# Re-ordering the weight loads of the first expert stage: earlier pieces for one unit, 0.9 MB more room for another

## The reference, cut to what matters

```python
for e in range(N_EXPERTS):                       # 32
    hid = jax.nn.silu(hf @ w_gate[e]) * (hf @ w_up[e])      # 1024 -> 256, twice
    y = y + (hid @ w_down[e]) * combine[:, e:e + 1]         # 256 -> 1024
```

## Time and profile before

| | us |
|---|---|
| median of three runs | 777.58 |
| lowest, highest | 776.46, 778.38 |
| the profiled execution, its own time | 776.66 |
| its span in the trace | 774.8 |
| outside the span (776.66 less 774.8) | 1.86 |

### The profile page before, as it was taken

One profiled execution on the slowest core, in us unless ns is written; L12 is line 12 of the kernel. 1 busy time (PEld: TensorE's weight loads), 2 busy tenths in 40 slices (PEclk: granted clock), 3 DMA queues, 4 the chain that ended last, 5 costly groups with the idle time before them and its releaser, 6 DMA issues.

```text
span 774.8 us, 16731 instructions
## 1 busy us (share of the span) xinstructions
PE 720.2 (93%) x7452; PEld 458.9 (59%) x7452; DVE 324.6 (42%) x688; ACT 206.7 (27%) x418; POOL 31.5 (4%) x99
## 2 busy tenths in 40 slices
PE   8999999999989998999999999999998997877796
PEld 6778787658645564554537745885765553343342
DVE  7476886635353323333236064633355331221222
ACT  2574568215100000000042363530330000100003
POOL 7006000000000000000000000000000000000000
PEclk9999999999999999999999999999999998898999
DMA  8644113399999999999999724359589999999995
GB/s 257 211 89 160 57 57 112 144 418 418 384 422 417 422 419 420 420 420 421 413 346 360 249 76 172 135 193 370 209 325 420 417 421 420 420 422 421 420 405 190
DMA packets 74871, 241.62 MB, mean 312 GB/s; under 512 B 10087, under 2 KB 39901, under 8 KB 55726
## 3 DMA queue, kind: packets, MB, share of 16 engines
q1 hardware_dynamic: 74590, 240.00, 80.1%
q10 hardware_dynamic: 208, 0.54, 0.2%
HBM read 239.48 MB, written 1.05 MB: 310 GB/s over the span
## 4 chain that ended last, share of the span: by engine, by line
PE 59%; DMA 15%; DVE 4%; issue 1%; SPq 1%; ACT 0%; ACTq 0%
PE ps L1588 11%; PE ps L1911 10%; DMA M<-in_m_w_up_dram 8%; PE ps L1424 7%; PE ps L1525 7%; PE ps L1667 5%; PE ps L1540 4%; DMA M<-in_m_w_down_dram 4%; DMA M<-in_m_w_gate_dram 3%; DVE H L2525 1%; PE ps L1063 1%; PE ps L1733 1%; PE ps L1805 1%; PE ps L1533 1%; PE ps L1459 1%
## 5 line engine op out<-in xcount | busy, mean ns | idle before, releaser
L1588 PE MATMUL ps<-M 128*32 128x256 f32 x2008 | 122.8, 393 | 15.7 <-DMA M<-in_m_w_gate_dram 8.8
L1588 PEld LDWEIGHTS ps<-M 128*32 128x32 f32 x2008 | 65.1, 113 | 70.5 <-issue 15.7
L1117 PE MATMUL ps<-M 128*128 128x272 f32 x352 | 85.3, 397 | 0.6 <-DMA M<-in_e_w_in_dram 0.6
L1911 PE MATMUL ps<-M 128*128 128x256 f32 (+2 forms) x288 | 79.9, 434 | 0.0
L1525 PEld LDWEIGHTS ps<-M 128*128 128x128 f32 x608 | 72.3, 194 | 12.7 <-issue 12.2
L1525 PE MATMUL ps<-M 128*128 128x128 f32 x608 | 77.8, 280 | 0.0
L1117 PEld LDWEIGHTS ps<-M 128*128 128x128 f32 x352 | 65.6, 190 | 15.9 <-issue 1.7
L1667 PE MATMUL ps<-M 128*32 128x512 f32 x448 | 59.6, 679 | 10.6 <-DMA M<-in_m_w_down_dram 10.6
L1911 PEld LDWEIGHTS ps<-M 128*128 128x128 f32 x288 | 53.7, 190 | 22.6 <-issue 15.6
L1540 PE MATMUL ps<-M 128*128 128x512 f32 (+1 forms) x120 | 60.4, 625 | 5.4 <-DVE H L2525 5.4
L2522 DVE TENSOR_TENSOR H<-H,ps 128x512 f32<-128x512 f32 x60 | 41.3, 688 | 49.2 <-PE ps L1540 48.9
(11 more groups left out here) (467 smaller groups left out, 851.7 us busy)
## 6 DMA issues: line engine op xcount, KB each, us to landing
M<-in_m_w_gate_dram SPq DMA_DIRECT2D x28, 2048.0 KB, 17.9
M<-in_m_w_up_dram SPq DMA_DIRECT2D x22, 2048.0 KB, 20.3
M<-in_m_w_down_dram SPq DMA_DIRECT2D x19, 2048.0 KB, 22.7
M<-in_m_w_down_dram SPq DMA_DIRECT2D x14, 1024.0 KB, 16.5
M<-in_o_w_in_dram SPq DMA_DIRECT2D x12, 1024.0 KB, 9.5
M<-in_e_w_in_dram SPq DMA_DIRECT2D x11, 1024.0 KB, 5.8
M<-in_m_w_gate_dram SPq DMA_DIRECT2D x9, 1024.0 KB, 6.9
M<-in_m_w_up_dram SPq DMA_DIRECT2D x8, 1024.0 KB, 18.8
```

Of the source, the lines that this page charges most:

```text
L1117: ins = pe.matmul(ps[:, n % 4, 0:T], wringE[:, (n // 2) % 4, k, (n % 2) * P:(n % 2) * P + P], (xnE if n else xuE)[:, k], start=(k == 0), s ...
L1588: ins = pe.matmul(ps[32 * e:32 * e + 32, 3 * x, 0:FF], xgT[q % 2][:, k, 32 * e:32 * e + 32], w, start=(k == 0), stop=(k == KD - 1))
L1911: ins = pe.matmul(ps[rows, unit % 4, 0:n], lhs(k), rhs(k), start=(k == 0), stop=(k == KD - 1))
```

## The change

It changes loads of the first expert stage, and with them where three tensors lie and which counts the waits of TensorE look for.

- **Pieces.** Of unit 2 (down weights of round 0, place 3) the first two experts are sent as four transfers of 0.5 MiB, each behind `oc_set` 1, 2, 3, 4. The last two experts stay behind `sa_evac` 5 and `lru_in` 6, as one transfer of 2 MiB.
- **A place of 0.5 MiB.** `aside[0]` gets a fourth entry: the first half of the up weights of the fourth expert of round 1 goes there, right behind those 2 MiB; before it went into place 1 behind `half_done` 1.
- **A place of 0.4 MB.** The level masks (`m_lev`) and the router weights (`wrr`) become parts of the tensor `K1`, which grows by what they had. `first_cols` (768 columns, 0.375 MiB) lies over the masks and the first layer's router weights; a transfer into it waits for `wrc_set` 1 (the router weights have been scaled into their own tensor, DVE line 2340). It takes the first three of the eight k slices of the first expert of unit 1. The part of place 2 that is free by this takes 0.375 MiB of the down weights of round 1 (unit 5) behind `res_done` 5.
- **What follows.** Behind `half_done` 1 go 2 MiB of unit 4 in two transfers; behind `gate_done` 1 the second halves of unit 8 (2 MiB, before 1.5 MiB behind `up_done` 1); behind `half_done` 2 only 0.125 MiB of unit 5; behind `up_done` 1 its second halves (2 MiB). Unit 8's first halves go as two transfers of 1 MiB.

```diff
-        aside = [[K0[:, 0:D], K1[:, 0:D], yst[1]], ...
+        aside = [[K0[:, 0:D], K1[:, 0:D], yst[1], at(36096, D)], ...
+        first_cols = K1[:, 1024:1024 + 3 * FF]
 # but_quarters (unit 1)
-                    sp.dma_start(slots[j][:, 0, :], src[:, 0, :]).then_inc(s(f"ld_s{j}"), 16)
+                    sp.dma_start(slots[j][:, 0, 3 * FF:2 * D], src[:, 0, 3 * FF:2 * D]).then_inc(s(f"ld_s{j}"), 16)
 ...
                 if y == 0:
+                    for c in range(4):
+                        e, h = divmod(c, 2)
+                        sp.wait_ge(s("oc_set"), c + 1)
+                        sp.dma_start(slots[3][:, e, D * h:D * h + D], down[:, e, D * h:D * h + D]).then_inc(s("ld_s3"), 16)
                     sp.wait_ge(s("sa_evac"), NC)
                     sp.wait_ge(s("lru_in"), 6)
-                    whole(2, down[:, 0:4])
+                    sp.dma_start(slots[3][:, 2:4, :], down[:, 2:4, :]).then_inc(s("ld_s3"), 16)
+                    set_aside(3)
 ...
 # unit 1, behind mixE 5
                             for e in range(2):
                                 set_aside(e)
+                            sp.wait_ge(s("wrc_set"), 1)
+                            sp.dma_start(first_cols, up[:, 0, 0:3 * FF]).then_inc(s("ld_pv_ys"), 16)
 # unit 3, behind res_done 5
+                            sp.dma_start(slots[UNIT_SLOT[y][5]][:, 0, 0:3 * FF], down[:, 4, 0:3 * FF]).then_inc(s("ld_lruw_e5"), 16)
 # unit 4
                             sp.wait_ge(s("half_done"), 1)
-                            sp.dma_start(slots[j][:, 3, 0:D], up[:, 7, 0:D]).then_inc(s("ld_half"), 16)
-                            sp.dma_start(slots[j][:, 0:3, 0:D], up[:, 4:7, D:2 * D]).then_inc(s(f"ld_s{j}"), 16)
+                            for e in (0, 2):
+                                sp.dma_start(slots[j][:, e:e + 2, 0:D], up[:, 4 + e:6 + e, D:2 * D]).then_inc(s(f"ld_s{j}"), 16)
                             wait_through(UNIT_PREV[y][u])
-                            sp.dma_start(slots[j][:, 3, D:2 * D], up[:, 7, D:2 * D]).then_inc(s(f"ld_s{j}"), 16)
+                            sp.dma_start(slots[UNIT_SLOT[y][8]][:, :, D:2 * D], down[:, 8:12, D:2 * D]).then_inc(s("ld_u8_lastk"), 16)
 # unit 5
                             sp.wait_ge(s("half_done"), 2)
-                            sp.dma_start(slots[j][:, 0, 0:D], down[:, 4, 0:D]).then_inc(s(f"ld_s{j}"), 16)
+                            sp.dma_start(slots[j][:, 0, 3 * FF:D], down[:, 4, 3 * FF:D]).then_inc(s(f"ld_s{j}"), 16)
                             wait_through(UNIT_PREV[y][u])
-                            sp.dma_start(slots[j][:, 0:3, D:2 * D], down[:, 4:7, D:2 * D]).then_inc(s(f"ld_s{j}"), 16)
-                            sp.dma_start(slots[j][:, 3, D:2 * D], down[:, 7, D:2 * D]).then_inc(s("ld_lruw_e5"), 16)
-                            sp.dma_start(slots[UNIT_SLOT[y][8]][:, 0:3, D:2 * D], down[:, 8:11, D:2 * D]).then_inc(s("ld_u8_lastk"), 16)
+                            sp.dma_start(slots[j][:, :, D:2 * D], down[:, 4:8, D:2 * D]).then_inc(s(f"ld_s{j}"), 16)
 ...
 # TensorE, half_gu
+                            elif u == 1 and y == 0 and k < 3 and e == 0:
+                                w = first_cols[:, FF * k:FF * k + FF]
```

More of the change, by code:

```diff
@@ L111, in program @@
         hsel, E2, cen, onesbd = K0[:, 640:672], K0[:, 672:800], K0[:, 800:928], K0[:, 928:1056]
-        K1 = sb("K1", [P, 1152])
+        K1 = sb("K1", [P, 2112])
         reset, gupO = K1[:, 0:640].bitcast(BF16), K1[:, 640:1152]
@@ L118, in program @@
         iota = sb("iota", [P, P])
-        m_lev = sb("m_lev", [P, 6, L])
+        m_lev = K1[:, 1152:1536].rearrange("p (l t) -> p l t", l=6)
         pv = sb("pv", [P, NPV])
@@ L126, in program @@
         dlast = sb("dlast", [P, 4, NC])
-        wrr = sb("wrr", [P, 2, KD, NG + NE])
+        wrr = K1[:, 1536:2112].rearrange("p (y k c) -> p y k c", y=2, k=KD)
         wrc = sb("wrc", [P, KD, NG + NE])
@@ L290, in program @@
         level, cmp = at(31616, NE, 8), at(31616 + 8 * NE, 16, NE)
-        aside = [[K0[:, 0:D], K1[:, 0:D], yst[1]], [K0[:, 0:D], K1[:, 0:D], at(26624, D), yst[1]]]
+        aside = [[K0[:, 0:D], K1[:, 0:D], yst[1], at(36096, D)], [K0[:, 0:D], K1[:, 0:D], at(26624, D), yst[1]]]
         apart = [H[:, 2, :], xgT[1].rearrange("p k t -> p (k t)"), at(33792, D), yst[0]]
         spare = at(36096, D)
+        first_cols = K1[:, 1024:1024 + 3 * FF]
         fn_row, fnb = K1[0:1, 0:D], K0[:, 0:D]
@@ L476, in experts @@
                         if y == 0:
-                            sp.dma_start(slots[j][:, 0:3, 0:D], down[:, 8:11, 0:D]).then_inc(s(f"ld_s{j}"), 16)
-                            sp.dma_start(slots[j][:, 3, :], down[:, 11, :]).then_inc(s(f"ld_s{j}"), 16)
+                            for e in (0, 2):
+                                sp.dma_start(slots[j][:, e:e + 2, 0:D], down[:, 8 + e:10 + e, 0:D]).then_inc(s(f"ld_s{j}"), 16)
                         else:
@@ L1557, in loaded @@
                     j = UNIT_SLOT[y][u]
+                    more = 48 if j == 3 else 0
                     if y == 0:
-                        pe.wait_ge(s(f"ld_s{j}"), 32 * (UNIT_TURN[y][u] + 1))
+                        pe.wait_ge(s(f"ld_s{j}"), 32 * (UNIT_TURN[y][u] + 1) + more)
                     else:
-                        pe.wait_ge(s(f"ld_s{j}"), 32 * FIRST_LAYER[j]
+                        pe.wait_ge(s(f"ld_s{j}"), 32 * FIRST_LAYER[j] + more
                                    + 16 * sum(TRANSFERS.get(x, 2) for x in range(u + 1) if UNIT_SLOT[1][x] == j))
                     if u == 1:
-                        pe.wait_ge(s("ld_pv_ys"), (304, 368)[y])
+                        pe.wait_ge(s("ld_pv_ys"), (320, 384)[y])
                     elif y == 0 and u == 3:
@@ L1581, in half_gu @@
                                 w = aside[y][e][:, FF * k:FF * k + FF]
-                            elif u == 4 and k >= KD // 2 and e < 3:
+                            elif u == 4 and k >= KD // 2 and (y == 0 or e < 3):
                                 w = gu_w[UNIT_SLOT[y][u]][:, e, k - KD // 2, :]
-                            elif u == 4 and k >= KD // 2 and y == 1:
+                            elif u == 4 and k >= KD // 2:
                                 w = spare[:, FF * (k - KD // 2):FF * (k - KD // 2) + FF]
+                            elif u == 1 and y == 0 and k < 3 and e == 0:
+                                w = first_cols[:, FF * k:FF * k + FF]
                             elif u == 1 and k < KD // 2 and e + y:
```

## The result

The changed kernel took 780.60 us (median of 18 runs, 777.72 to 785.71), the kernel before 777.53 (18 runs beside it, 776.04 to 780.38): a ratio of 1.0038 with a 95% interval of 1.0023 to 1.0053. It is slower, by 3.07 us, where 0.95 us faster was forecast, and the time lies outside the forecast range of 774.5 to 778.8.

The account below looks back on a forecast made before the run. Two paths were taken to end the first expert stage together: the weight stream and TensorE's own work. Removing waits of 0.75 and 0.20 us gives -0.95; 777.58 - 0.95 = 776.6 us, range 774.5 to 778.8.

Parts of the forecast that it names:

- So 2 MiB go into idle time: Chunk loop, 132 to 147 us: four pieces, 1.25 us each at 418 GB/s, fit where only 4 GB/s move.
- The mechanism: Rival, chance 0.08: four instruction loads at 132 to 147 us meet pieces, TensorE runs dry, up to 5.0 us lost.
- The argument against it: Against the instruction-load rival: from 150 to 195 us, at 418 GB/s, TensorE was busy 44.05 of 45 us.
- The fixed cost of 2 us a transfer: Skill page's cost beside the bytes; in the stream, four more transfers would cost 8 us. Restart rival: 782.6, chance 0.04.
- the lead: Weight stream of the first expert stage runs ahead by 1.7 to 2.6 us; 2.0 taken.
- The hole: Gap in the stream near 195 us, places full and waiting for TensorE; to grow from about 0.8 to 3.7 us.
- -0.95 us: Last round of the first expert stage: TensorE's waits for gate (0.75) and second half of up weights (0.20) go.
- No place is waited for longer: Behind the hole near 195 us, the changed byte order makes no wait for a place longer; nothing charged.
- TensorE's start at 193 us unmoved: Sign of being right: TensorE's expert work still starts at 193 us; later than 193.5 would be wrong.
- The second limit: Issue at 313.99 us, behind slow gate matmuls (6.26 instead of 3.66 us), caps the lead at 1.7 to 2.2 us.

Follow-up runs that it names:

- e1: The changed kernel without the early pieces: unit 2 whole behind `lru_in`, new places kept; 781.20 us, ratio 1.0029 to the kernel before.
- e4: The changed kernel with its four pieces as one transfer of 2 MiB behind `oc_set` 4; 778.04 us, ratio 1.0003 to the kernel before.
- e5: e4 without the `keep_busy(2, 3)` before the last gate weights of the first stage; 777.33 us, ratio 0.9986 to the kernel before.
- e6: The kernel before without the same `keep_busy` before the last gate weights; 777.95 us, ratio 0.9999 to the kernel before.
- e2: The kernel before with the four 0.5 MiB pieces alone, without the new places; 781.68 us, ratio 1.0055 to the kernel before.
- e3: The changed kernel with pieces of half the size, 0.25 MiB each, the rest behind `lru_in`; 781.58 us, ratio 1.0042 to the kernel before.
- e7: The changed kernel with four pieces of 32 KB, the rest behind `lru_in` 6; 783.52 us in one run.
- e8: The changed kernel with the 2 MiB as two pieces of 1 MiB, behind `oc_set` 1 and 3; 779.59 us in one run.

## Why the prediction was wrong

- **The step that failed is "So 2 MiB go into idle time".** The DMA engines were idle, but the pieces were costed at nothing on TensorE's path, while four instruction loads crossed that same time. With pieces the loop took 4.17 us longer, 3.7 to 3.8 of them the pieces' own (19.00 less 15.28, e1, or 15.18, e4).
- **The mechanism stood among the rivals, with a chance of 0.08.** Its prices, 779.1 for half and 781.6 for all, enclose the 780.60 measured. Its size was right by luck: a piece was put at 1.25 us of full rate and takes 2.4 us alone, and the stalls are 0.7 to 1.3 us each; that a block's work covers part of the delay is the likely reason.
- **The argument against it was read wrongly.** "In 150 to 195 us, at 418 GB/s, TensorE was busy 44.05 of 45 us": that stretch runs 500 instructions, two blocks at some 250, in 45 us. The loop runs 1036, four blocks, in 15. A late load is covered by 22 us of work there and by under 4 in the loop. The rows held this; "though with fewer instructions" should have been a division. Before, the cover was already used up: 0.3 us of "issue" stood in the loop.
- **The Trainium skill** bears on it in two places. Runtime: NRT & Kernel Launch, section Instruction fetch mechanics, says that instructions come in 16 KiB blocks of 256, fetched while the block before runs, at a cost "mostly hidden". The trace agrees on the block (253 by the count above) and on the hidden cost before, not after. DMA: Bandwidth & Descriptors, section Queues, rings and completion order, says that a DMA engine takes turns between queues only after a whole packet of several descriptors. A piece is 128 rows of 4 KB (13 for 0.05 MB in the row above), 8 for each of 16 engines if they are spread evenly, so by that rule a load may stand behind an engine's whole share of a piece. That the load comes with the piece's last bytes agrees. But the profile counts each of these rows as a packet, and if that is the page's packet a load would get its turn after one row; no view here shows the order on one engine, so why the load waits for all of a piece stays open. The fixed cost of 2 us a transfer that the prediction cites is stated there for transfers issued by GpSimd, and here SP issues them. No run here shows it in the stream.
- **Right: the lead.** The hole was to grow to 3.7 us: from 198 to 203 us 105 GB/s move, 5.0 x (1 - 105/418) = 3.7 us of missing traffic, 5 us later than forecast because TensorE is. The number agrees by luck: the stream starts 3.8 us later than before (150.48, 146.68) and the issue that ends the hole comes 5.6 later (200.70, 195.11), which by the prediction's arithmetic makes 5.5 us. That there is a lead is shown by the waits at the stage's end and by e5 against e6.
- **Right: -0.95 us.** Measured -1.12 from `keep_busy` to the last down weights. That TensorE comes 7 us later there is not the reason: in e2, without the new places, it comes 4.3 us later than before (382.51, 378.26) and both waits stay, 0.99 and 0.23 us. The stretch takes 17.15 or 17.16 us in all six kernels with the new places and `keep_busy` (after, e1, e3, e4, e7, e8), 18.28 before and 18.55 in e2.
- **"No place is waited for longer"** holds after, in e4 and in e8, where TensorE is late for other reasons. It hangs on the bytes of the pieces coming before `lru_in`: in e1, e3 and e7 the up weights of round 0 are 1.7 to 2.8 us late, and in e5, whose 2 MiB go out just ahead of it, 0.64. The prediction priced the new places by what they hold more, and not by what they put in front of round 0's up weights; that price is hidden only as long as the pieces pay it or TensorE is late.
- **"TensorE's start at 193 us unmoved"**, one of the prediction's own checks, failed: the start is at 198.71, where later than 193.5 was to be a sign of being wrong.
- **The second limit**, the slow stretch behind the extra pass, was there in every trace (the gate matmuls behind the pass take 5.2 to 6.3 us, at full clock 3.66), but moves: it costs 1.4 us more after than before, and no more in e5.

## What to carry to other kernels

In this kernel idle DMA engines were not free while TensorE ran many short instructions. So count the instructions of the stretch, divide by the block (some 250 here), and see how much work covers a late block. Keep bulk transfers out of such a stretch, or begin them so late that the last block of the stretch is already on its way (e4: last load of the loop at 145.2, first bytes at 145.6). "issue" in a row of waits, at intervals of one block, is the sign of it.

## What the runs showed of the hardware that was not expected

- A 0.5 MiB transfer alone took 2.4 us of moving bytes, half the rate of the full stream, and 3.8 us from issue to landing (the median of the four).
- TensorE resumed 2.2 to 2.5 us after a late load was listed in the kernel after, 2.4 to 2.6 in e2, e3 and e8. Against 3.2 to 4.2 us between two loads of the loop before, little is left for a delay.
- The granted clock fell for the same 24 matmuls in the kernel after and in e4 (4.54 us) and not in the other eight (2.92 us). e4 and e5 are the same program up to there, so it varies between executions; what sets it is open.
- Behind the stalls of 1.63 us (e2) and 2.08 us (e8) the granted clock was 0.50 for 6.8 us each; behind those of up to 1.32 us in the loop of the kernel after it stayed at 1.00. There a stall cost more than itself, some 2.5 us on top (an estimate from the same matmuls at either clock); each is one trace.
